# Two-layer decoder trunk: silus and convolved rows in another order in the first mixer, unread products around the first expert's transposes

## The reference, cut to what matters

```python
z = u @ w_in                                   # first mixer, u = rms_norm(h)
q, f, inp, g, gate_b, gate_c, h_b = jnp.split(z, AB_SPLITS, axis=-1)
forget = lb + (1.0 - lb) * jax.nn.sigmoid(f)
o_a = hgrn2_chunkwise(heads(silu(q)), heads(1.0 - forget), heads(inp), heads(log(forget)))
o_a = rms_norm(o_a, out_norm) * jax.nn.sigmoid(heads(g))
o_b = gate_b * causal_depthwise_conv(gate_c * h_b, conv_w)
mix = jnp.concatenate([o_a, o_b], axis=-1) @ w_out
...
for e in range(N_EXPERTS):                     # mixture of experts, 16 experts, top 2 in one group
    hidden = jax.nn.silu(xt @ w_gate[e]) * (xt @ w_up[e])
    y = y + combine[:, e:e + 1] * (hidden @ w_down[e])
```

## Time and profile before

| | |
|---|---|
| median of 3 runs | 1238.2 us (1238.01 to 1238.71) |
| profiled execution | 1236.09 us, span 1234.1 us |
| mean granted TensorE clock | 0.974 |
| PE busy | 1153.0 us (93%) |
| DVE busy | 877.0 us (71%) |
| ACT busy | 737.9 us (60%) |
| DMA | 279.71 MB, mean 227 GB/s |

### The profile page before, as it was taken

The page is one execution under the profiler, slowest core; times in us unless marked ns, Lnnn a source line. Parts: engine busy times, 40 slices in busy tenths (PEclk is TensorE's granted clock), DMA queues, the critical chain, the costliest instruction groups (busy, mean ns, idle before and its releaser), DMA issues. The chain is left out here.

```text
span 1234.1 us, 16709 instructions
## 1 busy us (share of the span) xinstructions
PE 1153.0 (93%) x5730; PEld 927.6 (75%) x5730; DVE 877.0 (71%) x1142; ACT 737.9 (60%) x906; POOL 135.4 (11%) x97
## 2 busy tenths in 40 slices
PE   6989999897799999999999998996899999999996
PEld 4768887686688888888668884684788888888575
DVE  5633345825699999999666438836699999999565
ACT  5533120223577887788656419733678788788664
POOL 0000000000121221121100000001021122121100
PEclk9989999899799999999999998998899999999999
DMA  9322212142499999999492211132599999999441
GB/s 379 123 69 86 85 35 69 39 166 103 161 367 375 376 382 381 375 372 390 159 383 85 91 47 35 69 136 106 198 353 389 380 376 385 379 376 382 169 168 69
DMA packets 48292, 279.71 MB, mean 227 GB/s; under 512 B 9344, under 2 KB 9344, under 8 KB 18928
## 3 DMA queue, kind: packets, MB, share of 16 engines
q1 hardware_dynamic: 34256, 243.06, 52.0%
q0 software_dynamic: 13984, 35.96, 7.7%
HBM read 272.68 MB, written 23.07 MB: 240 GB/s over the span
## 5 line engine op out<-in xcount | busy, mean ns | idle before, releaser
L1542 DVE TENSOR_TENSOR wlo<-raw,whi 128x2048 fp32r<-128x2048 f32 x213 | 485.9, 2290 | 108.6 <-ACT whi L1060 99.5
L431 PE MATMUL psum<-whi,ahi 128*128 128x512 f32 (+1 forms) x1184 | 473.8, 400 | 24.5 <-DVE alo L1746 5.8
L1060 ACT ACTIVATE whi<-raw 128x2048 fp32r<-128x2048 f32 (+1 forms) x215 | 409.6, 1907 | 89.6 <-PE psum L431 86.9
L431 PE MATMUL psum<-whi,alo 128*128 128x512 f32 (+1 forms) x1184 | 462.2, 390 | 0.0
L431 PE MATMUL psum<-wlo,ahi 128*128 128x512 f32 (+1 forms) x1184 | 461.7, 390 | 0.0
L431 PEld LDWEIGHTS psum<-whi,ahi 128*128 128x128 f32 x1184 | 224.9, 190 | 72.8 <-issue 19.6
L431 PEld LDWEIGHTS psum<-whi,alo 128*128 128x128 f32 x1184 | 224.6, 190 | 47.4
L431 PEld LDWEIGHTS psum<-wlo,ahi 128*128 128x128 f32 x1184 | 225.4, 190 | 41.6
L1060 ACT ACTIVATE arena<-psum 128x512 f32<-128x512 f32 (+1 forms) x145 | 82.9, 585 | 140.3 <-PE psum L431 111.1
L1060 ACT ACTIVATE ahi<-psum 128x512 fp32r<-128x512 f32 x140 | 78.6, 593 | 103.5 <-PE psum L734 61.6
L431 PE MATMUL psum<-arena 128*128 128x512 f32 (+8 forms) x794 | 121.3, 327 | 6.1 <-DVE arena L1861 4.4
(11 more groups left out here) (177 smaller groups left out, 818.5 us busy)
## 6 DMA issues: line engine op xcount, KB each, us to landing
raw<-w_moe_dram SPq DMA_DIRECT2D x192, 1024.0 KB, 9.3
raw<-w_dense_dram SPq DMA_DIRECT2D x35, 1024.0 KB, 7.8
arena<-yscr POOLq DMA_DIRECT2D x8, 1024.0 KB, 8.0
vscr<-arena POOLq DMA_DIRECT2D x8, 512.0 KB, 2.9
arena<-w_proj_dram POOLq DMA_DIRECT2D x2, 1024.0 KB, 5.9
arena<-gains_dram POOLq DMA_DIRECT2D x3, 512.0 KB, 3.6
out_dram<-arena SPq DMA_DIRECT2D x3, 512.0 KB, 2.6
h<-x_dram SPq DMA_DIRECT2D x2, 512.0 KB, 6.5
```

Source lines behind the costliest of these rows:

```text
L431: return nc.tensor.matmul(o, l, r, start=start, stop=stop, **kw)
L1060: return nc.scalar.activation(o, i, ACT.Copy, scale=scale)
L1542: tt(wlo[:, b % SPL, :], raw[:, b % RAW, :], halves(whi[:, b % SPL, :]), ALU.subtract).then_inc(lo_ready, 1)
```

## The change

In the first mixer, ScalarE does the silus of row tiles 0 to 2 between the exponentials of row tiles 2 and 3, and that of row tile 3 behind the last. The convolution has three buffers in place of two; `conv(0)` to `conv(2)` go with the tiles 1 to 3 of B's first chunk and `conv(3)` behind `gate(0)`. High and low parts of the convolved rows are made by row tile (all four feature tiles of 128 rows), alternating with those of the heads, and TensorE's tile q waits for q + 1 of them. VectorE's step `rec(22)` (output norm of the last row tile) goes behind the first two low parts. In `moe`, in both layers, TensorE does ten products whose result nobody reads behind the second index, and six behind the first expert's transposes.

```diff
@@ TensorE
-                    if i == 0 and q == 0 and k == BLK["out0"]:
-                        pe.wait_ge(g_blo, 4)
+                    if i == 0 and k == BLK["out0"]:
+                        pe.wait_ge(g_blo, q + 1)
...
+                def unread(n):
+                    for t in range(n):
+                        mm(PS[1][:, :], whi[:, B % SPL, 0:P], whi[:, B % SPL, 0:512], True, True)
+
                 index(0)
                 index(1)
+                unread(10)
                 x_T(0, 0, 0)
+                unread(6)
                 pe.wait_ge(h_ready, 3 * layer * TB + TB)
@@ ScalarE
+            def query(tb):
+                group_done(act, BLK["q"], tb)
+                nc.scalar.activation(Q[:, tb, :], PS[tb][:, :], ACT.Silu).then_inc(g_silu, 1)
...
                 nc.scalar.activation(yt, PS[5][:, :], ACT.Exp).then_inc(g_esf, 1)
+                if tb == TB - 2:
+                    for q in range(TB - 1):
+                        query(q)
             nc.scalar.activation(dec, PS[6][:, 0:64], ACT.Exp).then_inc(g_dec, 1)
-            splits(6)
-            for tb in range(TB):
-                group_done(act, BLK["q"], tb)
-                nc.scalar.activation(Q[:, tb, :], PS[tb][:, :], ACT.Silu).then_inc(g_silu, 1)
+            query(TB - 1)
             splits(7)
...
-            for ft in range(4):
-                act.wait_ge(g_ob, ft + 1)
-                if ft == 0:
-                    act.wait_ge(w_used, first_chunk(BLK["out0"]))
-                copy(ahi[:, 4 + ft, :], E[:, ft, :]).then_inc(g_bhi, 1)
-            splits(17)
-            for tb in range(TB):
+            def conv_hi(tb):
+                if tb == 0:
+                    act.wait_ge(g_ob, 4)
+                    act.wait_ge(w_used, first_chunk(BLK["out0"]))
+                copy(ahi[:, 4:8, tb * P:(tb + 1) * P], E[:, :, tb * P:(tb + 1) * P])\
+                    .then_inc(g_bhi, 1)
+
+            def heads_hi(tb):
                 act.wait_ge(g_oT, tb + 1)
                 copy(ahi[:, 0:4, tb * P:(tb + 1) * P],
                      PS[4 + tb % 2][:, :].rearrange("p (a b) -> p a b", a=4)).then_inc(g_mhi, 1)
+            conv_hi(0)
+            conv_hi(1)
+            heads_hi(0)
+            conv_hi(2)
+            heads_hi(1)
+            conv_hi(3)
+            splits(17)
+            heads_hi(2)
+            heads_hi(3)
@@ VectorE
+            def conv_out(ft):
+                return (yt, et, area(AR_Y3, 512), yt)[ft]
...
-                if ft >= 2:
-                    dve.wait_ge(g_ob, ft - 1)
+                if ft == 3:
+                    dve.wait_ge(g_ob, 1)
...
-                        if i == 0 and b == 2 and q >= 2:
-                            conv(q - 2)
+                        if i == 0 and b == 2 and q >= 1:
+                            conv(q - 1)
                         if i == 1 and b == 2:
                             gate(q)
-                            if q < 2:
-                                conv(q + 2)
-                        rec(b * 8 + i * 4 + q)
+                            if q == 0:
+                                conv(3)
+                        if b * 8 + i * 4 + q < 22:
+                            rec(b * 8 + i * 4 + q)
...
+            conv_lo(0)
+            conv_lo(1)
+            rec(22)
+            heads_lo(0)
+            conv_lo(2)
+            heads_lo(1)
+            conv_lo(3)
+            splits(17)
+            heads_lo(2)
+            heads_lo(3)
```

More of the change, by code:

```diff
@@ L95 @@
 AR_LBL, AR_LB = AR_Q, AR_ST
+AR_Y3 = 14848
 ARENA = 15360
@@ L1704, in rec @@
                     tt(G[:, t, :], K[:, t, :], G[:, t, :], ALU.mult).then_inc(g_oa, 1)
+            def conv_out(ft):
+                return (yt, et, area(AR_Y3, 512), yt)[ft]
             def conv(ft):
                 w = hc("convw")[:, ft * 3:ft * 3 + 3]
-                y = (yt, et)[ft % 2]
+                y = conv_out(ft)
                 if ft == 0:
@@ L1722, in gate @@
                 group_done(dve, BLK["B"], ft)
-                tt(E[:, ft, :], PS[ft][:, :], (yt, et)[ft % 2], ALU.mult).then_inc(g_ob, 1)
+                tt(E[:, ft, :], PS[ft][:, :], conv_out(ft), ALU.mult).then_inc(g_ob, 1)
             splits(8)
@@ L1735, in _, with conv_lo, heads_lo @@
                             tt(E[:, q, :], PS[q][:, :], E[:, q, :], ALU.mult).then_inc(g_H, 1)
-                        if i == 0 and b == 2 and q >= 2:
-                            conv(q - 2)
+                        if i == 0 and b == 2 and q >= 1:
+                            conv(q - 1)
                         if i == 1 and b == 2:
                             gate(q)
-                            if q < 2:
-                                conv(q + 2)
-                        rec(b * 8 + i * 4 + q)
[L1743 to L1746, removed]
+                            if q == 0:
+                                conv(3)
+                        if b * 8 + i * 4 + q < 22:
+                            rec(b * 8 + i * 4 + q)
+            def conv_lo(tb):
+                dve.wait_ge(g_bhi, tb + 1)
+                dve.wait_ge(g_ob, 4)
+                w = (slice(None), slice(4, 8), slice(tb * P, (tb + 1) * P))
+                tt(alo[w], E[:, :, tb * P:(tb + 1) * P], halves(ahi[w]), ALU.subtract)\
                     .then_inc(g_blo, 1)
-            splits(17)
-            for tb in range(TB):
+            def heads_lo(tb):
                 dve.wait_ge(g_mhi, tb + 1)
```

## The result

The changed kernel takes 1223.51 us (median of four runs, 1221.0 to 1225.13) against 1238.36: a ratio of 0.9878 with a 95% interval of 0.986 to 0.9897, 14.9 us or 1.2% faster. Beside the experiments it was timed once more: 1221.78 us against 1239.58, ratio 0.9854 (0.9837 to 0.9871). The forecast was 1221. The profiled execution took 1224.48 us with a span of 1222.5, against 1236.09 and 1234.1.

The account below looks back on a forecast made before the run. TensorE, 93% busy, was taken as the bound, through its waits and its time at the lower clock. 6.1 + 6.3 + 4.5 = 16.9 us took the profiled 1236.09 to 1219.2, the median to 1221; range 1217.5 to 1227.5.

Parts of the forecast that it names:

- Part A: First mixer, early silus: TensorE's 3.8 us wait ahead of the v block goes, plus 2.35 us of clock; 6.1 us.
- Part B: Ahead of the output projection, convolved rows by row tile: 4.5 us of waiting and 1.8 us of clock saved; 6.3 us.
- Part C: First experts of both layers: unread products bring the clock back before the first product; sum 4.9 us, taken as 4.5.
- the list of what is late next: Check behind the early silus and row tiles that each later input is in time; tightest slack 1 us for the rows.
- Rival 1: First experts: unread products do not lift the clock, 2.0 us lost, 1227.8 us; chance 0.20 with its mixed cases.
- Rival 3: Experts are bound by their loads, so the unread products give nothing: 1225.8 us; chance 0.05.
- Rivals 4 and 5: 4: clock low deep into first expert, 1254.6 us (0.02); 5: other waits behind each part, within 2.5 us of 1238.2 (0.02).

Follow-up runs that it names:

- e2: The kernel before with only the convolved rows by row tile (conv, gate, high and low parts): 1232.16 us, ratio 0.9936.
- e4: The kernel after without its unread products, so early silus and convolved rows together: 1224.70 us, ratio 0.9879 to the kernel before.
- e5: The kernel after again, unchanged, for a second trace: 1221.78 us, ratio 0.9854 to the kernel before.
- e6: The kernel after plus nine unread products in the gap at the experts' end, in both layers: 1220.34 us, ratio 0.9846 to the kernel before.
- e8: The kernel after with 18 transposes of 128x128 in place of the ten unread products: 1221.77 us, ratio 0.9856 to the kernel before.
- e12: The kernel after with every gap from router to first expert and at experts' end filled, plus 38 unread transposes ahead of the attention: 1218.91 us, ratio 0.9847.
- e3: The kernel before with only the ten and six unread products added: 1236.11 us, ratio 0.9976.
- e9: The kernel after without the six unread products behind the first expert's transposes: 1222.2 us, ratio 0.9871 to the kernel before.
- e10: The kernel after without the ten unread products ahead of the first expert's transposes: 1226.35 us, ratio 0.9904 to the kernel before.
- e7: The kernel before plus nine unread products in the gap at the experts' end and no others: 1237.17 us, ratio 0.998.
- e1: The kernel before with only ScalarE's early silus: 1232.36 us, ratio 0.9950.

## Why the prediction was right

- **Part A** was sized right: 6.1 us forecast, 6.2 (4.5 to 7.8) measured alone. Its idle time and its clock are both visible in one trace: from the sums' end to the transposes of k and q it takes 13.6 us after and 19.7 before, 6.1 less.
- **Part B** likewise: 6.3 forecast, 7.9 (6.2 to 9.5) alone. The remaining wait is 1.39 us where 1.3 was worked out, the last gate ends 0.9 us behind the start of the transposes (0.8 worked out), and no later tile waits. The clock stays up in the traces of after, e2, e4, e5, e6 and e8 to e12.
- **Part C** is where a size is off, by its net and not by its place. In the two first experts of the profiled pair the gain is 2.0 us (10.36 to 8.34) and 2.8 us (11.56 to 8.72), 4.9 together, against 4.9 in the sum and 4.5 taken. From first transpose to first product it saves 0.64 and 0.45 us (0.35 and 0.55 forecast), the rest is clock. Over the whole kernel it is less: 3.0 alone (1.6 to 4.3), and on top of silus and rows between nothing (0.9878 against e4's 0.9879) and 3 us (0.9854).
- The step that lacked a term was the list of what is late next. I asked it for waits and not for the clock: the 2.27 us gap at each experts' end was read as harmless because the trace of before had the clock at 1.00 there. Whether it falls there is a matter of the execution: e5 and the first trace of after are one kernel, with one fall and two. In the traces with unread products and that gap unfilled (after, e3, e5, e8, e9, e10) it fell at 7 of 12 ends, in those without at none of 8, while the time of e7 speaks for such falls in other executions of before. Why e10 and the first trace of after had both and e9 none is open, and so is whether unread products make them more frequent.
- The time taken for the profiled execution (1219.2) was 5.3 us too low, the one for the median (1221) 2.5 us too low in the first timing and 0.8 us too low in the second. Putting the same difference on profile and median assumed that the profiled execution of before was typical, which it was not. That the forecast comes within 0.8 us of the second median is in part luck: silus and rows gave 15.0 us where 12.4 were forecast, and the unread products less than their 4.5.
- Rival 1 (the clock not lifted) is out: the kernel after, e5, e8 and e9 have products 0.23 us apart from the first expert's first on. Its price was right in kind, as e10 shows: six products at 0.43 us hold the first product by 0.9 us. Rival 3 (loads) is out by e4 and by the waits in the experts; a late weight chunk outside the experts cost 1.2 us in the trace of after, and TensorE waits 1.0 us at the same place in that of e5. Rivals 4 and 5 did not come up.

## What to carry to other kernels

Price a gap of the tensor engine twice: its idle time, and half of the time that the products behind it run at the lower clock; for the two gaps here that was 3.8 + 2.35 and 4.5 + 1.8 us, and both came in. Work that nobody reads can buy the second part where the first can't be closed, but it must end before the awaited data arrive: ten products in a 4.3 us gap cost nothing, six products behind the transposes at the lower clock held the first product by 0.9 us per layer. After one and the same gap (here 2.3 us) the clock fell in some executions and not in others, so one trace does not tell its cost: look at the mean clock and the spread of all runs, or fill the gap and time that.

## What the runs showed of the hardware

float32 transposes of 128x128 alone brought the clock back, 6.0 us after their start in e8's first layer (297.52 to 303.5, with 0.45 us of waiting among them); in the second layer it was back 2.9 us after theirs (850.13 to 853.1). How long it takes is different from place to place: first experts without filler ran 3.0 to 5.7 us of products at 0.50 in before, e1, e2 and e4. Gaps of 1.4 us (output projection) and 1.69 us (e9) left it at 1.00 in every trace that had them; behind the 2.27 us one, and behind one of about 2 us in the first gated embedding, it fell in some traces and not in others (the latter: at 1.95 us in e2 and 1.89 in e8, but not at 1.95 in e10 or 2.09 in e5). From the same start of the program the clock first came up between 15.8 (e1) and 19.2 us (after).
